# A hybrid decoder step on one core: five dense token tiles instead of five and a quarter, gathered sample tokens packed, and gate rows made token by token on three engines

## The reference, cut to what matters

```
s = einsum('thcd,hcnd->thcn', q, sub_keys)
v1, i1 = top_k(s[:, :, 0], 16);  v2, i2 = top_k(s[:, :, 1], 16)
sc, sel = top_k(v1[..., :, None] + v2[..., None, :], 16)   # per head
expert = (i1 * 128 + i2)[sel];  g = softmax(sc)
a = einsum('td,thkd->thk', xb, u_tab[expert])
coef = g * gelu(a)
y = h + einsum('thk,thkd->td', coef, v_tab[expert])
```

## Time and profile before

| what | value |
|---|---|
| median of 3 runs | 4203.94 us (4201.71 to 4206.41) |
| the profiled execution | 4205.94 us, of which the span from first to last instruction is 4204.4 us |
| PE busy | 3381.9 us, 80% of the span |
| DVE busy | 2954.1 us, 70% |
| ACT busy / POOL busy | 1094.7 us, 26% / 1435.3 us, 34% |
| moved by DMA | 976.40 MB, mean 232 GB/s |
| chain that ended last | PE 45% of the span, all of it lines L1801 and L1814 |

### The profile page before, as it was taken

The page is one execution under the profiler, slowest core; times in us unless marked ns, Lnnn a source line. Parts: engine busy times, 40 slices in busy tenths (PEclk is TensorE's granted clock), DMA queues, the critical chain, the costliest instruction groups (busy, mean ns, idle before and its releaser), DMA issues. The chain is left out here.

```text
span 4204.4 us, 63555 instructions
## 1 busy us (share of the span) xinstructions
PE 3381.9 (80%) x22691; PEld 3015.0 (72%) x22691; DVE 2954.1 (70%) x6090; ACT 1094.7 (26%) x1891; POOL 1435.3 (34%) x1243
## 2 busy tenths in 40 slices
PE   7995669666555777725554999999999999999998
PEld 5874447333333555525554999999999999999998
DVE  6462443211120999988885888888888888988887
ACT  5442335221211222212222222222222222222221
POOL 0000000034420011116664445444454444545543
PEclk9998889787867888868887999999999999999999
DMA  3325722499976333412336999999999999989997
GB/s 133 108 80 176 268 61 62 164 367 387 350 266 228 102 134 128 138 43 90 127 127 237 316 311 309 305 305 316 322 306 305 308 312 312 309 303 312 311 310 244
DMA packets 494118, 976.40 MB, mean 232 GB/s; under 512 B 219370, under 2 KB 275820, under 8 KB 491388
## 3 DMA queue, kind: packets, MB, share of 16 engines
q0 software_dynamic: 140960, 563.49, 38.4%
q1 hardware_dynamic: 353012, 411.20, 28.9%
HBM read 881.29 MB, written 160.76 MB: 248 GB/s over the span
## 5 line engine op out<-in xcount | busy, mean ns | idle before, releaser
L1758 POOL DMA_INDIRECT uv_row<-in_v_rows,expert_tok x384 | 472.5, 1230 | 690.7 <-DVE y_tok L1927 659.8
L1801 PE MATMUL banks<-x_hi,u_hi 128*128 128x336 f32 x2048 | 647.5, 316 | 29.5 <-DVE u_lo L1880 29.5
L1814 PE MATMUL banks<-coef_hi,v_hi 128*128 128x336 f32 x2048 | 647.4, 316 | 4.5 <-issue 4.5
L1801 PE MATMUL banks<-x_hi,u_lo 128*128 128x336 f32 x2048 | 650.2, 317 | 0.0
L1814 PE MATMUL banks<-coef_hi,v_lo 128*128 128x336 f32 x2048 | 647.0, 316 | 0.0
L1801 PE MATMUL banks<-x_lo,u_hi 128*128 128x336 f32 x2048 | 646.4, 316 | 0.0
L1814 PE MATMUL banks<-coef_lo,v_hi 128*128 128x336 f32 x2048 | 645.8, 315 | 0.0
L1758 POOL DMA_INDIRECT uv_row<-in_u_rows,expert_tok x384 | 461.9, 1203 | 259.8 <-DVE dots L1908 203.5
L1927 DVE SCALAR_TENSOR_TENSOR y_tok<-uv_row,share,y_tok 128x1024 f32<-128x1024 f32 x384 | 491.1, 1279 | 0.5
L1908 DVE CUSTOM_DVE_ANT_0 uv_row<-uv_row,x_tok 128x1024 f32<-128x1024 f32 x384 | 468.1, 1220 | 0.0
L1801 PEld LDWEIGHTS banks<-x_hi,u_hi 128*128 128x128 f32 x2048 | 386.1, 189 | 29.7 <-issue 29.7
(11 more groups left out here) (250 smaller groups left out, 5707.9 us busy)
## 6 DMA issues: line engine op xcount, KB each, us to landing
keys_sa<-in_cache_k SPq DMA_DIRECT2D x256, 256.0 KB, 11.4
values_sa<-in_cache_v POOLq DMA_DIRECT2D x256, 256.0 KB, 6.6
uv_raw<-in_u SPq DMA_DIRECT2D x128, 512.0 KB, 6.6
uv_raw<-in_v SPq DMA_DIRECT2D x128, 512.0 KB, 6.7
scratch_gates<-stage SPq DMA_DIRECT2D x10, 4096.0 KB, 11.1
gates<-scratch_gates SPq DMA_DIRECT2D x128, 320.0 KB, 5.5
out_win_k_out<-in_state_k POOLq DMA_DIRECT2D x8, 4088.0 KB, 15.5
out_win_v_out<-in_state_v POOLq DMA_DIRECT2D x8, 4088.0 KB, 14.3
```

Of the source, the lines that this page charges most:

```text
L1758: pool.indirect_dma_start(out=rows[n % ROWS][:, :], out_offset=None, in_=io["u_rows" if kind == "u" else "v_rows"], in_offset=bass.Indirec ...
L1801: ins = nc.tensor.matmul(bank[:, 2 * r + c, 0:CH], u[r][a][:, k * P:(k + 1) * P], x2[b][:, k, c * CH:(c + 1) * CH], start=(k == 0 and a == b),
L1814: ins = nc.tensor.matmul(bank[:, 4 + n % 4, 0:CH], v[j][a][:, k * P:(k + 1) * P], coef[j][b][:, c * CH:(c + 1) * CH], start=(j == 0 and a ...
```

## The change

Names: `onehot_i` and `gated_i` are the two one-hot rows of a group, `picks_T` the picks turned to have tokens along the free dimension, `apart_squared` a squared distance, `uv_row` a fetched row.

- Dense tokens are now the first 640 (`DT = 5` tiles, `CH` = 320 columns); the gathered ones are the other 384 prompt tokens and the 32 sample tokens. The sample tokens' 128 picks are folded to 4 partitions a token (`PACK = 4`), so 32 more u and 32 more v units; a final small matmul sums the four partial rows of a token. An odd a slot holds 3 units, and there are 8 row buffers.
- Order of stages: prompt attention A, B, `mix_and_route` for the 8 prompt tiles, `spread_gates`, sample attention A, B, `mix_and_route` for the one sample tile, `run_experts`. The weights of `mix_and_route` are loaded twice, by ACT's DMA queue, during prompt attention B and sample attention B.
- `state_k` is moved during the first `mix_and_route`, `state_v` during `spread_gates`.
- `spread_gates`: 80 groups. DVE makes the first one-hot row of all 8 tokens with one operation, and for 5 tokens the gated row with one two-step operation each. ACT makes the other 3 gated rows: Square of the distance between place and key, then Relu of gate minus four times that. POOL computes nothing. `x2` is loaded and split at the start of `run_experts`.
- The gate table has 2560 bytes in a row for a block and a partition; it is stored in runs of 512 bytes and loaded by one DMA a block (before: two, with runs of 256 bytes).
- In `mix_and_route` both one-hot products are DVE's; the gathered tiles' rows are scaled there (`gain_rows`), which was done at the start of `run_experts`.

The core of the diff:

```diff
-GT = 3
-D0 = GT * P
-ND = NT - D0
+DT = 5
+ND = DT * P
+GT = SEQ // P - DT
+PACK = P // NS
@@ spread_gates, DVE
-                for c, row, ready in ((1, row2, plain_ready), (0, row1, places_ready)):
-                    nc.vector.tensor_tensor(row[g % RING][:, :, :], iota[:, :].unsqueeze(1).broadcast_to([P, E_GROUP, P]),
-                                            picksT[:, c, toks].unsqueeze(2).broadcast_to([P, E_GROUP, P]),
-                                            ALU.is_equal).then_inc(ready, 1)
+                nc.vector.tensor_tensor(row1[g % RING][:, :, :], iota[:, :].unsqueeze(1).broadcast_to([P, E_GROUP, P]),
+                                        picksT[:, 0, toks].unsqueeze(2).broadcast_to([P, E_GROUP, P]),
+                                        ALU.is_equal).then_inc(places_ready, 1)
+                for j in range(E_GROUP - BY_ACT):
+                    tok = slice(g * E_GROUP + j, g * E_GROUP + j + 1)
+                    ins = nc.vector.tensor_scalar(row2[g % RING][:, j, :], iota[:, :], picksT[:, 1, tok], picksT[:, 2, tok],
+                                                  ALU.is_equal, ALU.mult)
+                ins.then_inc(gated_ready, 1)
@@ spread_gates, POOL
-                nc.gpsimd.tensor_tensor(row2[g % RING][:, :, :], row2[g % RING][:, :, :],
-                                        picksT[:, 2, toks].unsqueeze(2).broadcast_to([P, E_GROUP, P]),
-                                        ALU.mult).then_inc(gated_ready, 1)
+            for b in range(DB):
+                since(pool, staged, b * (GROUPS // DB))
+                move_state(pool, io, 1, b, state_moved)
@@ spread_gates, ACT
+                for n, tok in enumerate(toks):
+                    ins = nc.scalar.activation(apart[:, g % 2, n, :], iota[:, :], ACT.Square, bias=neg_i2[:, tok])
+                ins.then_inc(apart_ready, 1)
+                act.wait_ge(apart_ready, g + 1)
+                for n, tok in enumerate(toks):
+                    ins = nc.scalar.activation(row2[g % RING][:, E_GROUP - BY_ACT + n, :], apart[:, g % 2, n, :], ACT.Relu,
+                                               bias=picksT[:, 2, tok], scale=-4.0)
+                ins.then_inc(act_gated, 1)
...
+            gated(0)
+            gated(1)
+            for g in range(GROUPS):
+                if g + 2 < GROUPS:
+                    gated(g + 2)
+                take(g)
@@ units_of_slots
-        n = 0 if slot == ("a", 0) else 2 if slot[0] == "a" else KD * TC
+        n = 0 if slot == ("a", 0) else 2 + slot[1] % 2 if slot[0] == "a" else KD * TC
@@ run_experts
-ROWS = 6
+ROWS = 8
...
+            load_x2(0)
+            load_x2(1)
             load_raw(0)
             load_raw(1)
-            load_gates(0)
+            for k in range(2, KD):
+                sp.wait_ge(x2_lo, k - 1)
+                load_x2(k)
@@ build
+                phase(attend_prompt, ident, bank, neg_lam, "b", weights)
+                phase(mix_and_route, ident, bank, weights, chosen, picksT, range(TILES - 1))
+            phase(spread_gates, bank, picksT)
+        phase(attend_sample, ident, bank, neg_lam, "a")
...
+            phase(attend_sample, ident, bank, neg_lam, "b", weights)
+            phase(mix_and_route, ident, bank, weights, chosen, None, range(TILES - 1, TILES))
+        phase(run_experts, bank, chosen)
```

More of the change, by code:

```diff
@@ L1049, with move_state, load_route_weights, mix_and_route @@
 PICKS = PH * TOPK
-def mix_and_route(nc, io, sems, ident, bank):
+def move_state(pool, io, which, b, moved):
+    state, out, new = (io[name] for name in (("state_k", "win_k_out", "kb"), ("state_v", "win_v_out", "vb"))[which])
+    kept = (STATE - DQ) * SEG
+    src, dst = state[b, :, :].rearrange("s c -> (s c)"), out[b, :, :].rearrange("s c -> (s c)")
+    pool.dma_start(dst[0:kept].rearrange("(a c) -> a c", a=64), src[DQ * SEG:].rearrange("(a c) -> a c", a=64)).then_inc(moved, 16)
+    pool.dma_start(out[b, STATE - DQ:, :], new[SEQ + b * DQ:SEQ + (b + 1) * DQ, :]).then_inc(moved, 16)
+def load_route_weights(act, io, weights, loaded):
+    w_out, w_q, sub_keys = weights
+    act.dma_start(w_out[:, :, :], io["w_out"].rearrange("(k p) c -> p k c", p=P)).then_inc(loaded, 16)
+    act.dma_start(w_q[:, :, :], io["w_q"].rearrange("(k p) c -> p k c", p=P)).then_inc(loaded, 16)
+    act.dma_start(sub_keys[:, :, :, :], io["sub_keys"]).then_inc(loaded, 16)
+def mix_and_route(nc, io, sems, ident, bank, weights, chosen, picksT, tiles):
     with ExitStack() as ctx:
         def sb(name, shape, dt=F32):
[L1059 to L1063, removed]
+            return ctx.enter_context(nc.sbuf_tensor(f"{name}_r{tiles[0]}", shape, dt))
+        def sem(name):
+            return sems(f"{name}_r{tiles[0]}")
+        w_out, w_q, sub_keys = weights
         iota = sb("iota_sb", [P, P])
         g2T = sb("g2_T", [P, KD])
+        g2_rows = sb("g2_rows", [P, D])
         subln = sb("subln_sb", [P, 1])
@@ L1107, in mix_and_route @@
[L1107 to L1119, removed]
@@ L1156, in _ @@
[L1156 to L1172, removed]
@@ L1830, in _ @@
             outputs(SUPER - 1)
+            pe.wait_ge(fold_loaded, 16)
+            pe.wait_ge(unit_done, len(units))
+            for c in range(2):
+                nc.tensor.matmul(bank[0:NS, c, :], fold[:, :], y_tok[GT % 2][:, c * 512:(c + 1) * 512],
+                                 start=True, stop=True).then_inc(y_folded, 1)
         @block.scalar
@@ L1925, in add_row @@
                 dve.wait_ge(share_ready, grp + 1)
[L1926 to L1928 removed]
+                out, row, by = y_tok[q % 2][:, :], rows[n % ROWS][:, :], share[:, grp % 2, i % GROUP:i % GROUP + 1]
+                if i == GT * P:
+                    nc.vector.tensor_scalar(out, row, by, None, ALU.mult).then_inc(unit_done, 1)
+                else:
+                    nc.vector.scalar_tensor_tensor(out, row, by, out, ALU.mult, ALU.add).then_inc(unit_done, 1)
             def unit(n):
@@ L2119 @@
         io[name] = nc.dram_tensor(f"scratch_{name}", shape, F32).ap()
+    for name, shape in UINT_SCRATCH.items():
+        io[name] = nc.dram_tensor(f"scratch_{name}", shape, U32).ap()
     build(nc, io)
```

710 lines of the change are left out of this document (372 added, 338 removed).

## The result

The changed kernel takes 4030.1 us, median of 4 runs (4029.6 to 4033.7); the kernel before, beside it, 4205.2 (4201.7 to 4207.1). The ratio is 0.9586, 95% interval 0.957 to 0.9603: 175 us faster, where 154 were forecast; 4030 lies in the range and 20 us under the forecast of 4050. The profiled execution has a span of 4028.3 us, 176.1 less than before.

What follows compares the result with a forecast made beforehand. PE's matmul columns bound the experts, a ring of POOL and DVE the spreading. Terms: -82 + 7 + 16 - 131 - 35 + 11 + 24 - 84 + 120 = -154, giving 4050 us; range 3985 to 4115.

Steps and rivals of the forecast that it cites:

- Experts, columns: Expert stage: 12288 matmuls of 320 columns instead of 336, 147.1 ns each instead of 153.8: -82 us.
- DMA in the experts, +16: Expert stage: DMA's nearly full share makes a turn 57.0 us instead of 56.5, over 32 turns: +16 us.
- Start of the experts, +7: Expert stage: the x2 loads and splits coming to its start, and the last fold, cost +7 us (-10 to +20).
- Spreading, -131: Spreading: ACT sets 2.7 us a group; with DMA queueing, the tail and the start, 259 us instead of 389.9.
- 10 us of queueing: Spreading: allowance because DMA's 220 us for table and state copies equal what ACT needs: +10 us.
- the old ring: Spreading before the change: POOL and DVE wait for each other, read as 4.64 us a group.
- the twin row: Spreading before the change: DVE's other row of the same shape, 1212 ns against the gated row's 2730.
- Mix stage, -84: First mix stage: earlier start -20, one tile fewer -56, DVE's product -12, scaling +4: -84 us.
- Sample tile, +120: Second mix stage: the sample tile pays for a stage of its own, +120 us (110 to 135).
- sample attention B, +24: Sample attention B: 9.4 MB of weights compete with the stage's own loads, +24 us (9 to 32).
- Prompt attention A, -35: Prompt attention A: losing eight 4-MB state copies saves 11 us at the start and 24 later, -35 us.
- B, +11: Prompt attention B: 9.4 MB of weights loaded beside its first loads cost +11 us (0 to 27).

Runs made afterwards that it cites:

- gates_twice: The changed kernel with each block's gates loaded a second time into an unread tile, and seven row buffers instead of eight: 4030.8 us.
- rows_6: The changed kernel with six buffers for fetched rows instead of eight: 4036.9 us.

## Why the prediction was right, and where its sizes were off

**Experts, columns.** Right: 147.2 ns a matmul, -82, and DVE just keeps up, as the comparison of 55.9 with 56.5 us a turn had it.

**DMA in the experts, +16: the term that failed.** It took a fetch's 1.52 us of the engines as a fixed cost, added up a share of 0.98 and charged a quarter of what 0.94 would cost (0.5 of 2.1 us a turn). The share of busy engines is no such capacity: with two more units a turn a fetch took 1.43, the share went from 0.91 to 0.93, and gates_twice carried 365 GB/s at 0.97 with PE busy throughout. The term was worth nothing; at 0 the forecast would have been 4034.

**Start of the experts, +7.** The stage less PE's busy time is 42.1 us, before 41.2: about +1.

**Spreading, -131.** Right in mechanism, 7 us too much. A group takes 2.80, not 2.7, as an ACTIVATE in a row adds 0.30 where the prediction's row gave 0.26 (those eight read PSUM and were scaled, these read SBUF and have a bias; which of the two makes it was not tried). 80 groups are 224. The 10 us of queueing came as 7.1 us of ACT's waits for stores. The tail is 31 us instead of 27, with nothing else on the DMA engines: the last tile went at 270 GB/s, not at the 333 read off a burst of 2.6 us, whose DMA share of 1.12 says that the window was too short for a rate. The reading of the old ring as 4.64 us a group was wrong (3.97, and x2's waits), and did no harm since the new time was built from its own parts. So was the remark that the twin row is "not made beside POOL": it does run beside POOL, but starts first.

**Mix stage, -84.** The start gained 25 instead of 20: the selection begins 58.7 us after the stage's start (83.5 before). A tile's period is (1215.86 - 828.26) / 7 = 55.4, 1.0 less, which is what -12 for the product and +4 for the scaling make over eight tiles; the end gained 5 that was not in the sum.

```profile
828.26 0.06 DVE L1413 MEMSET gate_r<- 128x1 f32 x1
...
1215.86 0.06 DVE L1413 MEMSET gate_r<- 128x1 f32 x1
```

**Sample tile, +120, and sample attention B, +24.** 120.0 and 22.6. The prediction's lower end of 9 does not follow from the figures beside it: 32 us less 18% of 102.7 leave 13.5.

**Prompt attention A, -35, and B, +11.** -36.7; B +17.8, nearer the end of 27 at which all weights pass first.

**The total.** 22 us below the sum's 4052 are -36 of stages that went better than forecast (the experts and the mix stage first) and +14 of two that went worse (spreading and prompt attention B), so part of the closeness is luck.

**The rivals.** Not one took place: DMA did not bind the experts, ACT's operations overlap, PE's clock was 0.91 of full speed in the spreading (the lower of its two levels, 1.2 of 2.4 GHz, is 0.5), POOL was the cause of DVE's 2730 ns, and fetches were no longer with eight in flight.

## What to carry to other kernels

Before an elementwise operation goes to POOL to spare DVE, look whether DVE's operations that start behind it wait for its end (here 2890 ns instead of 1215); taking POOL's back made the stage 45 us faster. A busy share of 0.9 of DMA is not a tenth of room or a lack of it: the only way found to know was to add traffic and look for waits. An early load is free only behind the loads that the stage itself waits for, and a stage for one tile costs its whole chain, here twice its place in a pipeline.

## What was not expected of the hardware

Eight fetches in flight cost a fetch less of the engines' time (1.43 us) than six did in the kernel before (1.52), at the same bytes; rows_6 with six again has 1.44 (66.9% of 1700 us over 413.46 MB), so it is not the buffers that did it, and the cause is open. The gates' loads changed between the two kernels as well, from 217853 packets for 175.80 MB on q1 to 51848 for 165.20, and no run changes them alone. Five small DVE operations with a value from each partition took 1.37 us, about 0.26 for each further one, though each is listed with 351 ns.
